# A weight ring that starts 128 and 256 bytes further on in SBUF

## The reference

```python
h = rmsnorm(x)
conv_val, conv_gate, pool_in, gate_a, gate_b = split(h @ w_in + b_in)     # 1024 -> 5 x 1024
ya = silu(layernorm(causal_dwconv31(conv_val * sigmoid(conv_gate)))) @ conv_w_out
yb = grouped_linear(trailing_means(pool_in) - pool_in) * pool_scale       # windows 2, 4, 8, 16
x = x + (sigmoid(gate_a) * ya + sigmoid(gate_b) * yb) @ mix_w_out
u = causal_dwconv3(rmsnorm(x) @ w_up)                                     # 1024 -> 5632
x = x + (gelu(u[:2816]) * u[2816:]) @ w_down
return rmsnorm(x)
```

## Time and profile before

| | before |
|---|---|
| median of 3 runs | 1288.99 us (1288.68 to 1289.66) |
| profiled execution | 1289.33 us, of which the span 1287.3 us |
| mean granted TensorE clock | 0.998 of full |
| TensorE busy (matmuls) | 1270.3 us, 99% |
| weight loads busy | 1053.8 us, 82% |
| VectorE, GpSimd, ScalarE busy | 1022.8, 871.1, 479.5 us |
| chain that ended last | 90% TensorE |
| DMA | 179.26 MB, mean 139 GB/s |

### The profile page before, as it was taken

One profiled execution on the slowest core, in us unless ns is written; L12 is line 12 of the kernel. 1 busy time (PEld: TensorE's weight loads), 2 busy tenths in 40 slices (PEclk: granted clock), 3 DMA queues, 4 the chain that ended last, 5 costly groups with the idle time before them and its releaser, 6 DMA issues.

```text
span 1287.3 us, 15571 instructions
## 1 busy us (share of the span) xinstructions
PE 1270.3 (99%) x5766; PEld 1053.8 (82%) x5766; DVE 1022.8 (79%) x1163; ACT 479.5 (37%) x691; POOL 871.1 (68%) x579
## 2 busy tenths in 40 slices
PE   8999999999999999999999999999999999999997
PEld 8888888888888778877888888888888888888887
DVE  5898989999999784589677767677666779887975
ACT  6211221213234580143445343343344445424551
POOL 4536637665787833478739977877887876567861
PEclk9999999999999999999999999999999999999999
DMA  9411121214334372344212322332232259868923
GB/s 352 149 33 49 34 82 49 82 33 164 99 99 149 130 290 69 114 155 164 102 39 90 123 107 92 121 121 88 93 117 107 90 175 361 332 243 290 367 87 131
DMA packets 66408, 179.26 MB, mean 139 GB/s; under 512 B 4896, under 2 KB 13088, under 8 KB 62496
## 3 DMA queue, kind: packets, MB, share of 16 engines
q1 hardware_dynamic: 61888, 167.82, 36.2%
q10 hardware_dynamic: 4448, 10.49, 2.2%
HBM read 137.14 MB, written 41.16 MB: 139 GB/s over the span
## 4 chain that ended last, share of the span: by engine, by line
PE 90%; DVE 4%; ACT 2%; issue 2%; POOL 1%; DMA 1%; SPq 0%; DVEq 0%; POOLq 0%; ACTq 0%
PE ps L2494 30%; PE ps L2495 30%; PE ps L2496 30%; DMA cv<-in_x 1%; DVE h_lo L2092 1%; POOL w_lo L1037 1%; PE ps L2558 1%; ACT cv L1244 0%; PE ps L2548 0%; DVE cv L2083 0%; ACT cv_r L1626 0%; DVE hi_f L2004 0%; POOL w_lo L1170 0%; DVE res L2271 0%; DVE res L2187 0%
## 5 line engine op out<-in xcount | busy, mean ns | idle before, releaser
L2494 PE MATMUL ps<-h_lo,w_hi 128*128 128x512 f32 (+1 forms) x900 | 348.0, 387 | 4.5 <-DVE h_lo L1838 1.9
L2496 PE MATMUL ps<-h_hi,w_hi 128*128 128x512 f32 (+1 forms) x900 | 345.9, 384 | 0.0
L2495 PE MATMUL ps<-h_hi,w_lo 128*128 128x512 f32 (+1 forms) x900 | 345.9, 384 | 0.0
L2494 PEld LDWEIGHTS ps<-h_lo,w_hi 128*128 128x128 f32 x900 | 169.0, 188 | 41.8 <-DVE h_lo L1838 3.1
L2496 PEld LDWEIGHTS ps<-h_hi,w_hi 128*128 128x128 f32 x900 | 169.0, 188 | 33.9
L2495 PEld LDWEIGHTS ps<-h_hi,w_lo 128*128 128x128 f32 x900 | 169.1, 188 | 33.1
L1918 DVE SCALAR_TENSOR_TENSOR ps<-tmp,par,ps 128x512 f32<-128x512 f32 x224 | 158.5, 750 | 0.0
L965 POOL TENSOR_SCALAR w_hi<-raw 128x1024 fp32r<-128x1024 f32 x32 | 36.5, 1141 | 156.1 <-issue 127.5
L2494 PE MATMUL ps<-ga_r,w_hi 128*128 128x512 f32 (+1 forms) x303 | 117.4, 388 | 0.3 <-POOL w_lo L1170 0.3
L2496 PE MATMUL ps<-cv_r,w_hi 128*128 128x512 f32 (+1 forms) x303 | 117.1, 386 | 0.0
L2495 PE MATMUL ps<-cv_r,w_lo 128*128 128x512 f32 (+1 forms) x303 | 117.0, 386 | 0.0
(11 more groups left out here) (308 smaller groups left out, 2721.3 us busy)
## 6 DMA issues: line engine op xcount, KB each, us to landing
raw<-in_wstream SPq DMA_DIRECT2D x54, 512.0 KB, 3.5
tmp<-in_wffn SPq DMA_DIRECT2D x14, 1024.0 KB, 4.7
g_kept<-res SPq DMA_DIRECT2D x21, 512.0 KB, 2.8
res<-in_wffn SPq DMA_DIRECT2D x10, 1024.0 KB, 4.8
ga_r<-g_kept SPq DMA_DIRECT2D x18, 512.0 KB, 7.0
h_lo<-g_kept SPq DMA_DIRECT2D x17, 512.0 KB, 7.5
res<-in_xT SPq DMA_DIRECT2D x7, 1024.0 KB, 5.8
g_kept<-raw SPq DMA_DIRECT2D x12, 512.0 KB, 2.9
```

Source lines behind the costliest of these rows:

```text
L2494: nc.tensor.matmul(out, a_hi, b_lo, start=start, stop=False, skip_group_check=onto)
L2495: nc.tensor.matmul(out, a_lo, b_hi, start=False, stop=False, skip_group_check=onto)
L2496: return nc.tensor.matmul(out, a_hi, b_hi, start=False, stop=stop, skip_group_check=onto)
```

## The change

Three allocations without a use are added: 32 float32 columns (128 bytes for each partition) ahead of `w_hi`, as many ahead of `w_lo`, and 64 ahead of `tmp`. `w_hi` and `w_lo` are allocated in the same order as before. No instruction, semaphore or transfer is changed other than in the addresses that it names.

```diff
--- before.py
+++ after.py
@@ -322,7 +322,12 @@
         cv, cv_r = two_views("cv", "cv_r", TS)
         ga, ga_r = two_views("ga", "ga_r", TS)
         raw = sb("raw", 2 * CH)
-        w_hi, w_lo = sb("w_hi", 2 * CH, f32r), sb("w_lo", 2 * CH, f32r)
+        LINE = P // 4
+        sb("ahead_of_w_hi", LINE)
+        w_hi = sb("w_hi", 2 * CH, f32r)
+        sb("ahead_of_w_lo", LINE)
+        w_lo = sb("w_lo", 2 * CH, f32r)
+        sb("ahead_of_tmp", 2 * LINE)
         GLW = 2 * (PAD + HALF)
         tmp = sb("tmp", 2 * GLW + 2 * SEQ + WPAD)
         par = sb("par", NPAR)
```

## The result

The changed kernel takes 1312.83 us, the median of 4 runs (1312.56 to 1313.44), against 1289.24 us of the kernel before beside it (1288.68 to 1289.66): a ratio of 1.0184 with a 95% interval of 1.0166 to 1.0202. It is 23.6 us slower, where 1289.0 was forecast. The profiled execution has a span of 1311.0 us.

What follows compares the result with a forecast made beforehand. TensorE, 99% busy, was taken as the bound: number of matmuls times their spacing, plus some ten microseconds. Nothing added or removed and all address prices 0 left the median of the runs, 1289.0 us, range 1286.8 to 1291.4.

Steps and rivals of the forecast that it cites:

- points 2 and 3 of the sum: Weight loads from w_hi and w_lo, and other engines writing these tiles: both taken as 0, with +1.7 and -2.2 us for the range.
- the ring: The tiles w_hi and w_lo, stationary operand of 3945 of 5766 matmuls; predicted to move by 128 and 256 bytes.
- point 1: Spacing of the 3945 matmuls with stationary operand in w_hi or w_lo: 0 ns, though every nanosecond would be 3.9 us.
- Rival (a): TensorE's fixed 13.4 ns per matmul is an address collision that the shift removes: 52.9 us less, 1236.4 us; chance 0.10.
- Rival (b): Loads of shifted w_hi and w_lo tiles cross an aligned 512-byte block: up to 4 ns each, 15.8 us, 1304.8 us; chance 0.07.
- the common remainder: The remainder of 512 bytes at which the big tiles, raw, w_hi, w_lo and tmp all start before the change.
- the 4 ns of the earlier trace: Gap between median weight loads, 188 ns from w_hi and w_lo, 192 ns from ones at another remainder; taken as hidden.
- Rival (c): The unused allocations might be dropped, leaving w_hi and w_lo in place: time unchanged at 1289.0 us; chance 0.03.
- The rules set against the row: Skill pages against TensorE's 13.4 ns: independent read ports give 0; a fixed 2.5 ns leaves 10.9 unexplained, 43 us if removed.
- the likeliest case: Whole kernel: time stays within the noise, 2.6 us either way; chance 0.83.

Runs made afterwards that it cites:

- all128: Against the kernel before, all tiles moved together by 128 bytes, so differences between tiles stay; 1288.54 us (ratio 0.9994).
- whi256: Against the kernel before, w_hi alone plus 256 bytes, with w_lo and tmp 512 bytes on; 1289.48 us (ratio 1.0002).
- first sweep: Kernel before with blocks of 16 matmuls (w_hi weights, h_hi moving) appended at varied start offsets, two blocks in bfloat16; 1361.97 us, one profiled execution.
- wlo128: Against the kernel before, w_lo alone plus 128 bytes, tmp 512 bytes on; 1304.50 us (ratio 1.0119).
- both192: Against the kernel before, w_hi and w_lo both plus 192 bytes, tmp 512 bytes on; 1297.21 us (ratio 1.0060).
- run 229: Not a follow-up run: "run" is a verb here, and 229 is a matmul step in ns within both192.

## Why the prediction was wrong, point by point

**What bounds the kernel** was right: TensorE's spacing times its matmuls. Its busy time grew by 24.6 us, the span by 23.7. That no engine but TensorE would see the addresses was right as well; points 2 and 3 of the sum (loads, filling the ring) came out at 0.

**The step that failed** is point 1, the price of a matmul whose ring tile has another remainder, taken as 0 ns with the sentence that the trace has no such pair. It is 6.6 ns on the 3801 ring matmuls of 512 columns, 25 us; on the 144 of 256 columns, which the sum counted alike, it is nothing. Two arguments for the 0 were wrong in themselves. The measured period is 256 bytes, so weights at the four multiples of 512 all agree with the moving tile, and their equal spacing says nothing on other offsets. And "the price never varies, not even where a matmul came late" is not what the trace of before says. After each late start it varies for several steps. The timeline of before, from 430.77 us, behind a wait for GpSimd:

```profile
430.77 0.47 PE L2494 MATMUL ps<-res_r,w_hi 128*128 128x512 f32 x1 [1.49 <-POOL w_lo L1037]
431.08 0.40 PE L2495 MATMUL ps<-ga_r,w_lo 128*128 128x512 f32 x1
431.31 0.40 PE L2496 MATMUL ps<-ga_r,w_hi 128*128 128x512 f32 x1
...
433.16 0.39 PE L2495 MATMUL ps<-ga_r,w_lo 128*128 128x512 f32 x1
433.39 0.39 PE L2496 MATMUL ps<-ga_r,w_hi 128*128 128x512 f32 x1
```

From 431.08 to 433.16 us are nine steps, by the starts in nanoseconds 2087 ns: 231.9 ns each, and only then do they settle at 226.7. I had read the spacing in the middle of a long undisturbed stretch, where it is in its good state. The starts in nanoseconds have 151 steps of 229 to 260 ns among 5350, and 145 of them lie within ten steps of such a place. A neighbour was there for the unknown price: the bad state of the same matmul, on average 5 and at most 9 ns above the good one. By the mean of these nine steps the price is 3945 x (231.9 - 226.7) = 20 us, 1309 us in all; by the highest of them, 236 ns, it is 37 us. A range built on this row would have reached from one to the other, and the 1312.8 lie there. That the unsettled state and the disagreement of tiles are one thing is not shown; it would have been an estimate.

**Rival (a)** had the right variable, the relative start of the moving tile and the weights, and the wrong sign: the kernel before was already in the best relation that any run here showed for 512 columns. (Its 1236.4 us are counted from the profiled execution; from the median of 1289.0 they are 1236.1.) What it made of 13.3 ns = 32 columns = 128 bytes, is not borne out: no placement gained anything beyond the noise, and the surplus of float32r went under 32 cycles with no offset and no load size at 512 columns. **Rival (b)** had the sign, and a price (15.8 us) of the right order, from a wrong mechanism: the loads kept their 188 ns although the ring had left the common remainder, so the 4 ns of the earlier trace rows were no matter of the address, and all128 and whi256 make ring tiles cross the old grid of 512 bytes for nothing. **Rival (c)** was refuted by the groups: only those with ring weights grew.

**The rules set against the row.** bfloat16 shows 215.8 ns, 2.5 over the 213.3 of its columns; float32r has 226.7 at best. The trace agrees with the fixed 2.5 ns of the Trainium skill, page "TensorE: Matmul & The Clock Gate", section "Wait — 56ns, not 53.3ns?", for bfloat16 and not for float32r. The Trainium skill, page "SBUF — State Buffer", section "Who interferes with whom", lets no other engine contend with TensorE, and none had a part in the sweep's slow blocks. It also calls TensorE's two read ports independent. By that the relative start of the two reads should not matter, and for float32r with 512 columns it does: it is worth 6.6 ns here. The measurement decides, though it doesn't show at which place the two meet.

**The range** of 1286.8 to 1291.4 was built on the likeliest case alone, and its bounds came from the durations of other engines, and nothing in them covered the one price that had not been measured. The unknown term multiplied by 3945 had to carry the range.

**What stays open.** Why the two reads interact is not settled. The trace only shows that an agreeing pair falls into a regular step of 544 cycles after some 3 to 10 matmuls, and that a disagreeing one runs in irregular or alternating steps (229 and 237 ns at plus 128 in the first sweep) with a mean of up to 560, at plus 96 bytes 562. That this is a matter of phase between the two reads is argued and not shown; nor is it explained why plus 192 costs 7 us where plus 128 costs 20, why 248 bytes cost what 240 and 252 don't (each is one block of 16 in one run), why a smaller load costs more, or why the price goes with fewer moving columns. Whether the 26 cycles that float32r has at best over bfloat16 are a part of the same interaction is open too.

## What to carry to other kernels

Where TensorE is the bound with float32r matmuls of 512 columns, let the weight tile and the moving tile of each matmul start at the same remainder of 256 bytes; padding the weight buffers by 32, 64 or 128 bytes cost 1.6 to 1.8% here, and moving all of them together cost nothing. Before putting a price of 0 on something the trace "never shows", look for the same instruction in its disturbed state, right behind the waits: its spacing there is the nearest row. And a term that multiplies with thousands of instructions sets the width of the range, however unlikely it looks.

## What the runs showed of the hardware that I had not expected

- The spacing of float32r matmuls of 512 columns depends on the start of the weights relative to the moving tile, with a period of 256 bytes: 226.7 ns at 0 and 256, 233.3 at 32, 64 and 224, 232.5 (both tiles of the ring) or 233.3 (one pair) at 128.
- The dependence is neither smooth nor in steps of 32 bytes: 4 bytes past agreement cost 13 cycles, 4 and 16 bytes short of it none, 8 bytes short 16.
- In wlo128 a disagreeing weight tile slows two steps, its load's and its use's (232.5 and 234.1 ns, the third 226.8). Elsewhere the slow steps spread: where every step has the same relation (both192), they run 229, 232, 226 ns.
- In bfloat16 there is none of it: 215.8 ns at both offsets. With 256 moving columns in float32r the offset costs nothing either (119 ns over both blocks, 120 aligned and 118.8 shifted once settled).
- Smaller weight loads don't make float32r matmuls faster: 32 weight columns have 44 surplus cycles, 128 have 32, both aligned.
- After a late start an aligned stream needs 2 to 9 further steps, of up to 240 ns, until it settles at 226.7.
